# Side jobs that take four PSUM banks in turn in the first kind of block, and two of four in the attention, instead of one bank of their own

## The reference

```python
y_a, v_first = rwkv7_time_mix(ps, vl, v_first, ...)
y_b = multiscale_pool(z_pool, pool_w[l], pool_scale[l])
mixed = br_gate[:, :, 0] * (y_a @ proj_a[l]) + br_gate[:, :, 1] * (y_b @ proj_b[l])
x = x + gt1 * (mixed @ w_out[l])
h2 = rms_norm(x, norm2_g[l]) * (1 + sc2) + sh2
x = x + gt2 * ((jax.nn.silu(gate) * up) @ w_down[l])
```

```python
branch_a = (o_gla * jax.nn.silu(gg)) @ w_o_gla
branch_b = gqa_attention(q, k, v) @ w_o_attn
mixed = jax.nn.sigmoid(gate_a) * branch_a + jax.nn.sigmoid(gate_b) * branch_b
h = h + rms_norm_2(mixed @ w_out, g_mix_post)
```

## Time and profile before

| | |
|---|---|
| median of three executions | 4382.35 us |
| the profiled execution | 4382.11 us |
| its span, first to last instruction | 4380.3 us |
| PE busy | 3946.5 us (90%) |
| DVE busy | 1987.6 us (45%) |
| ACT busy | 858.8 us (20%) |
| POOL busy | 2254.4 us (51%) |
| mean granted clock of PE | 0.950 |

### The profile page before, as it was taken

The page is one execution under the profiler, slowest core; times in us unless marked ns, Lnnn a source line. Parts: engine busy times, 40 slices in busy tenths (PEclk is TensorE's granted clock), DMA queues, the critical chain, the costliest instruction groups (busy, mean ns, idle before and its releaser), DMA issues.

```text
span 4380.3 us, 48456 instructions
## 1 busy us (share of the span) xinstructions
PE 3946.5 (90%) x18868; PEld 3184.4 (73%) x18868; DVE 1987.6 (45%) x2679; ACT 858.8 (20%) x1331; POOL 2254.4 (51%) x2214
## 2 busy tenths in 40 slices
PE   6589989999789989999997889999998879899997
PEld 4478768887578767888776657788787666578886
DVE  6963365454854373122344465412344535652124
ACT  2211111001311111001322242100132313420002
POOL 4331087787421086775543435577655433357773
PEclk9799999999899999998998999899989989989998
DMA  5321134453110133332222213233322221223331
GB/s 217 125 80 30 46 125 150 156 174 127 53 46 30 46 123 89 96 97 75 80 70 70 75 49 96 73 97 98 97 68 70 65 82 56 63 82 96 97 96 60
DMA packets 186274, 385.98 MB, mean 88 GB/s; under 512 B 20800, under 2 KB 20928, under 8 KB 179264
## 3 DMA queue, kind: packets, MB, share of 16 engines
q1 hardware_dynamic: 163728, 337.71, 24.8%
q10 hardware_dynamic: 22320, 45.18, 3.0%
HBM read 361.84 MB, written 20.97 MB: 87 GB/s over the span
## 4 chain that ended last, share of the span: by engine, by line
PE 75%; DVE 18%; ACT 4%; issue 2%; DMA 1%; ACTq 0%; SPq 0%; DVEq 0%
PE psum L373 16%; PE psum L375 16%; PE psum L374 16%; PE psum L514 2%; PE psum L440 2%; PE psum L533 2%; PE psum L526 2%; PE psum L393 1%; PE psum L418 1%; PE psum L394 1%; PE psum L395 1%; PE psum L842 1%; DVE units L1667 1%; PE psum L420 1%; PE psum L419 1%
## 5 line engine op out<-in xcount | busy, mean ns | idle before, releaser
L2034 POOL TENSOR_SCALAR w_hi<-raw 128x512 fp32r<-128x512 f32 x1080 | 754.2, 698 | 1755.9 <-DMA raw<-weight_chunks 1754.0
L2036 POOL TENSOR_TENSOR w_lo<-raw,w_hi 128x512 fp32r<-128x512 f32 x1080 | 1466.2, 1358 | 90.1
L373 PE MATMUL psum<-in_hi,w_hi 128*128 128x512 f32 x1968 | 790.1, 401 | 50.8 <-ACT zbuf L1004 31.2
L374 PE MATMUL psum<-in_lo,w_hi 128*128 128x512 f32 x1968 | 774.4, 393 | 0.0
L375 PE MATMUL psum<-in_hi,w_lo 128*128 128x512 f32 x1968 | 773.4, 393 | 0.0
L373 PEld LDWEIGHTS psum<-in_hi,w_hi 128*128 128x128 f32 x1968 | 375.2, 191 | 150.0 <-ACT zbuf L1004 35.9
L374 PEld LDWEIGHTS psum<-in_lo,w_hi 128*128 128x128 f32 x1968 | 375.2, 191 | 84.2 <-issue 7.3
L375 PEld LDWEIGHTS psum<-in_hi,w_lo 128*128 128x128 f32 x1968 | 374.6, 190 | 79.7
L418 PE MATMUL psum<-in_hi,w_hi 128*128 128x512 f32 x576 | 268.4, 466 | 32.0 <-ACT gate_st L978 25.6
L419 PE MATMUL psum<-in_lo,w_hi 128*128 128x512 f32 x576 | 231.5, 402 | 0.0
L420 PE MATMUL psum<-in_hi,w_lo 128*128 128x512 f32 x576 | 231.3, 402 | 0.0
(11 more groups left out here) (393 smaller groups left out, 7109.2 us busy)
## 6 DMA issues: line engine op xcount, KB each, us to landing
raw<-weight_chunks SPq DMA_DIRECT2D x1080, 256.0 KB, 2.6
ada_at<-ada_slabs SPq DMA_DIRECT2D x48, 1024.0 KB, 4.9
spill<-gate_st ACTq DMA_DIRECT2D x56, 256.0 KB, 2.7
gin<-spill ACTq DMA_DIRECT2D x32, 256.0 KB, 3.1
mgs<-spill ACTq DMA_DIRECT2D x32, 256.0 KB, 2.7
sml<-small ACTq DMA_DIRECT2D x4, 1024.0 KB, 6.4
spill<-nt ACTq DMA_DIRECT2D x16, 256.0 KB, 2.6
x<-x_in SPq DMA_DIRECT2D x1, 2048.0 KB, 29.8
```

The costliest lines, as they stand in the source:

```text
L373: pe.matmul(bank[:], wh, hi[:, i, :], start=(i == 0), stop=False)
L374: pe.matmul(bank[:], wh, lo[:, i, :], start=False, stop=False)
L2034: ts(w_hi[:, slot, :], raw[:, slot, :], 1.0, 1.0, ALU.mult, ALU.mult).then_inc(sem("chunk_hi"), 1)
L2036: ins = tt(w_lo[:, slot, :], raw[:, slot, :], w_hi[:, slot, :].bitcast(F32), ALU.subtract)
```

## The change

The pools become lists of banks that the program replaces as it goes on. A bank's uses are counted over all pools, so that `begin` waits for every earlier reader of the bank, whichever pool it belonged to.

- In a block of the first kind, from the start of the preparation to the end of the last `fill`, side jobs take banks 0, 1, 2 and 3 in turn. No projection of `lin` is begun in that stretch. Then `bg` goes back to bank 3.
- In the softmax attention, `lin` has banks 0 and 1, and side jobs take banks 2 and 3 in turn. Then both go back.
- In the gated linear attention nothing changes, and no instruction other than the waits changes anywhere: the order on every engine and in the stream of weights stays.

```diff
-        BANKS = {"lin": (0, 3), "bg": (3, 1), "aux": (4, 4)}
+        bank_uses = [0] * 8
+        banks_of = {"lin": (0, 1, 2), "bg": (3,), "aux": (4, 5, 6, 7)}
...
             def begin(name, pool):
                 n = used[pool]
-                first, banks = BANKS[pool]
-                b, uses = first + n % banks, n // banks
+                b = banks_of[pool][n % len(banks_of[pool])]
+                uses = bank_uses[b]
+                bank_uses[b] += 1
                 if uses:
                     pe.wait_ge(sem(f"bank{b}_read"), uses)
...
+                banks_of["bg"] = (0, 1, 2, 3)
                 fill(FILL_PREP)
...
                 fill(4 * DT * (2 * DT + 4))
+                banks_of["bg"] = (3,)
                 for m in range(DT):
                     projection(("pa", l, m), "proj_a", l, m, ...)
...
                 side_jobs([(("g2b", l, m), "w_in2", l, N_GB + m) for m in range(DT)])
+                banks_of["lin"], banks_of["bg"] = (0, 1), (2, 3)
                 for i in range(KVH):
                     projection(("k", l, i), "w_in2", l, N_AK + i, h_in)
...
                 fill(DT * DT)
+                banks_of["lin"], banks_of["bg"] = (0, 1, 2), (3,)
                 for m in range(DT):
                     projection(("p2b", l, m), "w_o_attn", l, m, ...)
```

## The result

| | before | changed |
|---|---|---|
| median of 11 executions each, us | 4383.94 (4377.46 to 4390.58) | 4391.78 (4388.30 to 4400.08) |
| ratio | | 1.0021 [1.0013, 1.0030] |
| ratio, second group of runs | | 1.0012 [1.0001, 1.0022] |
| profiled execution, us | 4382.11 | 4388.30 |

The account below looks back on a forecast made before the run. PE was taken to bound the kernel, on the chain of waits for 75% of it (DVE 18%). Terms of +1.0, +0.5, -1.4 and -0.2 summed to -0.1 us, so 4382.0 us, range 4371 to 4389.

Parts of the forecast that it names:

- The waits: Side jobs' bank waits at L418 fall from 32 us to about 8; PE waits longer at L480, L434 and L777.
- The waits for `yt`: Norm over heads: PE waits longer for DVE's `yt` at L434, by 0.7 us for each d from 1 on.
- the recurrence: None of the 16 waits lies in its chunks, whose length stays the same: gain nothing.
- First preparation: First block: PE's 8 us lead becomes idle time, then transposes and first scores start at low clock: +1.0 us (-1.3 to +2).
- Second preparation: Second block: PE's earlier jobs win time, collisions and low clock cost some: +0.5 us in sum (-3.5 to +5).
- collisions: Second preparation: dense PE frees chunks sooner, POOL's splits slow DVE by 1.2 us per chunk: +3.6 us.
- the clock: Second preparation: PE's low clock at the transposes costs up to 1 us, taken as +0.4 us.
- PE's lateness: Second preparation: DVE idled 4.83 us before `units`, 1.29 of which stay, so at most 3.5 us can be won.
- Norm over heads: Wait between `mean` and `var` goes in d=0, the chain moves up: gain 0.69 us per block, 1.4 in all (0 to 5.8).
- Attention: Softmax attention: bank waits become waits for `qn`; gain 0.1 us per layer, 0.2 us in all (0 to 6.4).
- The rival on the clock: PE's clock falls to 0.50 at side jobs: 4660 us for all 56, 4410 us for a tenth; chance 0.01.
- DVE pays for PE's haste: POOL's splits gather in DVE's busiest stretches; ten more collisions and two low-clock starts of 2 us each: 4394 us, chance 0.05.

Follow-up runs that it names:

- e2: Kernel before, with four banks in turn only from the end of the recurrence to the last side job (norm over heads): 4383.42 us, ratio 1.0003.
- e10: Kernel before, with four banks and POOL's weight splits deferred until DVE's memset is done, in the second block's preparation only: 4374.37 us, ratio 0.9980.
- e6: Kernel before with its one bank, POOL's splits behind each preparation's eight chunks deferred until DVE's memset is done: 4379.81 us, ratio 0.9993.
- e8: Kernel before, with four banks in both preparations only and POOL's splits behind their eight chunks deferred until DVE's memset is done: 4371.69 us, ratio 0.9973.
- w3: e8 plus the change in the softmax attention (two banks for projections, two for side jobs): 4378.11 us, ratio 0.9979 to the kernel before.
- w1: Changed kernel plus 8 unused matmuls ahead of the wait for `qn` of the attention's second key head: 4391.38 us, ratio 1.0013 to the kernel before.

## Why the prediction was wrong

**The waits.** Right in the main. L420's waits ended at 6.6 us for the forecast 8, one of 4.3 for `zbuf` among them; L482 waits 8.1 us per block for DVE, forecast 7. The waits for `yt` were mis-sized: 0.7 us more each was forecast, and six of them grew by 10.4 us, 1.7 each. That nearly all 30 us would come back as other waits was right. So was the recurrence: from its first state to its last it took 144.3 and 144.0 us in the changed kernel, 144.6 and 144.2 before.

**First preparation.** Forecast +1.0 us. The start of `units` behind `bonus` grew by 1.5 us at the low clock, outside the 1 us that the prediction allowed; 1.0 came back in `mt`, and by the first state +0.1 us was left in the profiled pair. The means of six traces with four banks and five with one are 102.3 and 102.4 us from the first V product to that state. The term is nothing, within its bounds.

**Second preparation: mis-sized.** The term was +0.5 us, from -3.5 for PE, +3.6 for collisions and +0.4 for the clock. The means of six traces with four banks (33.9 to 37.6) and five with one (33.0 to 34.9) are 36.4 and 33.8 us: +2.6 us, and +3.1 us by the first state. The collisions were sized rightly: DVE's stretch to `bonus` grew by 4.0 us in the profiled pair and by 2.9 in the means. The other two items, from `bonus` to `units`, were -3.1 together in the sum and are -0.3 in the means (5.27 less 5.57 us). PE's lateness is the one that failed: the profiled kernel before had DVE idle for 4.83 us before `units`, but in three of the other four traces with one bank this was 1.3 us. There, PE had not been the late one, so there was nothing to win, and the mean to be won was 1.4 us, not 3.5. One execution stood for all. The Trainium skill ("SBUF — State Buffer", section "SBUF: two separate sides") has an exclusive lock on the ports that both engines use; the alternation of 0.98 and 1.66 us, against 0.69 and 0.75 us, agrees with it in kind. It does not agree in size: one of POOL's pairs and two of DVE's instructions took 2.7 us together, where one behind the other they would take 3.3 (1.89 and 1.42), so the 1.2 us for each chunk in the sum was a better price than the rule of the Trainium skill gives. 9.9 us of DVE's 30.0 us hung on these collisions.

**Norm over heads: failed.** Forecast -1.4 us. The step "so the whole chain behind it moves up by 0.69 us" holds for the chain's start alone: DVE then met POOL's splits at other instructions, and the gain was gone by the next `yt`. From DVE's first product behind `mean` to its first with `pa` the first block took 77.8, 79.2, 78.3, 76.7 and 77.6 us in five traces with recurrence and norm changed, and 74.5 to 75.7 in five with neither or with the recurrence alone; 75.9 with the norm alone (e2). But e10, whose first block is unchanged, shows 78.3 too, and e6, e8 and w3, where POOL is deferred and the norm has one bank, 77.4, 78.3 and 77.0, so the longer course comes without four banks too. Part of it returns behind: to the first product of the feed-forward (`hs`) the same five and five took 187.4 and 186.1 us in the mean in the first block, 190.4 and 189.6 in the second, +1.3 and +0.8 us. So no gain of 1.4 us is in the traces; what of the loss is the change's stays open.

**Attention: failed.** Forecast -0.2 us. The step "The wait becomes one for `qn`, and 0.1 us is left" was right in kind and left out its price: one wait of 2.4 to 2.8 us in place of two shorter ones drops the clock, about 1.6 us in each layer by the traces, 3.1 us in all. The rival on the clock was put aside with "No wait is added, so no row speaks for it": a wait need not be added, it is enough that two merge. That the fall costs these 1.6 us is argued from the traces; filling the wait (w1) gave no gain in time. The Trainium skill ("TensorE: Matmul & The Clock Gate", section "A second HAM failure mode: psum-queue depth-cycling") blames the cycling through banks for short idle moments that move the clock; here cycling removed short moments, and the longer wait behind them moved it.

**The rival "DVE pays for PE's haste"** had the right mechanism. That its 4394 us come near 4392 is luck: it needed ten more collisions at 1.2 us and 4 us of cold starts, where the second preparation had 2.9 us of collisions in the means and the cold starts nothing in the first block and at most some 1.2 us in the second. Its sum is wrong as well, since ten collisions are 12 us and not 10. It got a chance of 0.05 because -3.5 and +3.6 cancelled in the second preparation.

**The sum.** Nothing for the first preparation, +3.1 for the second, +2.1 for the norm and +3.1 for the attention give some 8 us, and 5 to 9 us were measured. That the parts add up so is an argument, not shown: no single part was resolved by its times. The granted clock goes with it: its mean over the executions was 0.9472 and 0.9483 for the changed kernel in its two groups, 0.9505 to 0.9512 for the kernel before in four. Within the sixteen programs (174 executions) 0.001 less clock went with 2.0 us more, so 0.003 would be 6 us; since both kernels with extra matmuls raised the clock (0.9497, 0.9489) and not the speed, it is a companion of the idle time rather than its whole price. The range also failed by its own width: eleven or twelve executions of one program spread over 9 to 17 us, and three runs had shown 4.4.

## What to carry to other kernels

Before a wait is taken away, ask what ends next and what the earlier release sets off: here the bank and DVE's collisions with POOL had to be dealt with together, worth 12 us, while each alone gave nothing that could be measured. When two short waits merge into a long one, look whether PE's clock falls behind it. Where an idle time in one trace carries a term, look for the same place in a second execution first.

## What the runs showed of the hardware

In e8 POOL's pair for one chunk came every 1.94 us beside DVE's `bonus` and `units`, which read PSUM, and neither engine was slower for it:

```profile
1221.60 0.62 POOL L2044 TENSOR_SCALAR w_hi<-raw 128x512 fp32r<-128x512 f32 x1
1222.31 1.27 POOL L2046 TENSOR_TENSOR w_lo<-raw,w_hi 128x512 fp32r<-128x512 f32 x1
```

Beside DVE instructions with both inputs in SBUF it came every 2.7 us (1.06 and 1.60 us), and two such DVE instructions went from 1.42 us to 2.64 us.

PE's clock fell behind every one of eleven waits of 2.36 us and more at the second key head and behind none of 1.77 us or less there; at another place, the last head, an idle time of 2.37 to 2.39 us had a fall in 12 of 34 cases, so the length of a wait alone does not decide it.

Executions of the unchanged kernel within one group differed by up to 19 us, their clocks lying between 0.948 and 0.954.
